# Six extra products on TensorE behind the fourth up-projection slab, in two layers and a third block

## The chip, the cores and the metric

The kernel runs on one NeuronCore of one Trainium2 chip, as one program. The metric is the device time of one execution in microseconds (us); where several executions were timed, their median is given.

## What is computed

The reference is a chain of three transformer blocks on 256 tokens of width 1024, all in 32-bit floats. The first block function runs its layer twice; the second one runs a different layer once, which the kernel calls the third block. Cut to what matters for the change:

```python
def first_block(x, mem, ...):
    for l in range(2):
        a = hybrid_mixer(rms_norm(x, pre_mix_g[l]), ...)
        x = x + rms_norm(a, post_mix_g[l])
        c = memory_cross_attention(rms_norm(x, pre_xattn_g[l]), rms_norm(mem, mem_g[l]), ...)
        x = x + rms_norm(c, post_xattn_g[l])
        hdn = jnp.square(jax.nn.relu(rms_norm(x, pre_mlp_g[l]) @ w_up[l]))      # 1024 -> 4096
        x = x + rms_norm(hdn @ w_down[l], post_mlp_g[l])                        # 4096 -> 1024
    return x

def second_block(x, mem, ...):
    ...
    h = rms_norm_2(x, norm_ffn_g[0])
    x = x + jnp.square(jax.nn.relu(h @ w_ff1[0])) @ w_ff2[0]                    # 1024 -> 4096 -> 1024
    return x
```

## The kernel before

Activations lie transposed: channels on the 128 partitions in eight chunks, the 256 tokens along the row. A weight matrix comes in slabs of 1 MB, 2048 floats on each partition, which are mostly eight 128-row chunks of 256 columns. There are 64 slabs to a layer and 59 in the third block. Slabs 32 to 47 of a layer are the up-projection and 48 to 63 the down-projection; in the third block these are 27 to 42 and 43 to 58.

To keep near 32-bit accuracy at the speed of the rounded type (F32R), each slab is split in two parts. SyncE loads the slab into one of two buffers `raw`, and waits for the low part of the slab two before. ScalarE copies it rounded into `w_hi` (`split_hi`, L504, the copy at L514), for which it waits until TensorE has done with the slab three before, since `w_hi` and `w_lo` are rings of three. VectorE writes the rest into `w_lo` (`split_lo`, L524). When that is done, the semaphore `slab_lo` is raised. The activations are split in the same way (`act_hi` and `act_lo`, for the hidden layer `h_hi` and `h_lo`, for an attention's output `o_hi` and `o_lo`).

TensorE then makes three products for each pair of chunks, high by high, high by low and low by high (`products3`, L560 to L562, within `columns_slab`; L2199, L2201 and L2203 for a down-projection slab). Each is one weight load of 128x128 and one product that streams 256 columns. A slab has 2 column halves x 8 chunks x 3 = 48 of them.

```python
def products3(pe, o, stat_hi, stat_lo, mov_hi, mov_lo, first, last):
    pe.matmul(o, stat_hi, mov_hi, start=first, stop=False)
    pe.matmul(o, stat_hi, mov_lo, start=False, stop=False)
    return pe.matmul(o, stat_lo, mov_hi, start=False, stop=last)
```

TensorE's program is in one order, written out by hand: `TE_ORDER` for a layer and `TE_ORDER_2` for the third block. In a layer the piece that matters here reads: slabs 28 to 31 (the last projection of the cross attention), `stat` 4, `pair` 32 (slabs 32 and 33 interleaved chunk by chunk, L603, L605 and L611), `stat` 5 (sums for the norm, L2061), and then slabs 34 to 63 without anything between them, and `stat` 6 (L2046). In the third block it is `pair` 27, `stat` 2, slabs 29 to 50, `out` 0 (four transposes of the result, L2378), slabs 51 to 54, `out` 1, slabs 55 to 58, `out` 2 and 3. Each item opens a bank of PSUM by `open_bank` (L542), which waits until the reader of the bank's use eight before has emptied it; the fifth up-projection slab writes the bank called `up4`.

Ahead of some items `keep_clock` (L2015, from the tables `WARM` and `WARM_2`) puts products whose result nobody reads. They multiply the identity by constants, both from the tile `cst`, in plain 32-bit floats, not in F32R:

```python
pe.matmul(b[:, 0:T], ident, cst[:, 0:T], start=True, stop=True)
```

VectorE scales an up-projection bank (L1444, `probs`), ScalarE squares it and rounds it (L929, L930), and VectorE writes `h_lo` (L1450).

Of the kernel before, what the change touches and what calls it, by code (L numbers as in the profile page):

```python
# [16 lines left out]
P = 128  # L17
T = 256
# [4 lines left out]
DEPTH = 2  # L23
# [295 lines left out]
def build(nc, A, out):  # L319
    ctx = ExitStack()  # L320
    with ctx:
        def sem(name):
            return ctx.enter_context(nc.semaphore(name))

        def sb(name, shape, dt=F32, on=ctx):
            return on.enter_context(nc.sbuf_tensor(name, shape, dt))
# [3 lines left out]
        w_hi = sb("w_hi", [P, RING, SLAB], F32R)  # L330
# [47 lines left out]
        sig = {name: sem(name) for name in PER}  # L378
# [17 lines left out]
        def value(name, layer, n):  # L396
            return layer * PER[name] + (n + (PER[name] if name in CREDIT else 0))
# [103 lines left out]
        def slot(layer, s):  # L501
            return (64 * layer + s) % RING
# [14 lines left out]
        def split_lo(dve, layer, s):  # L517

            dve.wait_ge(sig["slab_hi"], value("slab_hi", layer, s + 1))
            sp = s if s < 64 else 0  # L520
            pieces = split_views_2 if second(layer) else split_views
            for (d, r), (h, _) in zip(pieces(sp, w_lo[:, slot(layer, s)], raw[:, s % RAW]),
                                      pieces(sp, w_hi[:, slot(layer, s)], raw[:, s % RAW])):
                ins = dve.tensor_tensor(d, r, h.bitcast(F32), ALU.subtract)  # L524
            ins.then_inc(sig["slab_lo"], 1)
# [9 lines left out]
        def second(layer):  # L535

            return isinstance(layer, int) and layer == DEPTH

        def bank(use, layer=0):
            return banks[(INDEX_2 if second(layer) else INDEX)[use] % N_BANKS]  # L540

        def open_bank(pe, layer, use):  # L542

            n = (INDEX_2 if second(layer) else INDEX)[use] - N_BANKS
            if second(layer) and n >= 0:
                _, name, count = USES_2[n]
                if name in once:
                    pe.wait_ge(once[name], count)
                else:
                    pe.wait_ge(sig[name], value(name, DEPTH, count))  # L550
                return bank(use, layer)
            while USES[n % NU] is None:
                n -= N_BANKS
            _, name, count = USES[n % NU]
            pe.wait_ge(sig[name], value(name, layer, count - (PER[name] if n < 0 else 0)))
            return bank(use, layer)
# [1423 lines left out]
        def _(pe):  # L1980
# [21 lines left out]
            for l in range(DEPTH):  # L2002
# [5 lines left out]
                      start=True, stop=True).then_inc(i_turned, 1)  # L2008
# [6 lines left out]
            def keep_clock(layer, use, n):  # L2015

                b = open_bank(pe, layer, use)
                for _ in range(n):
                    pe.matmul(b[:, 0:T], ident, cst[:, 0:T], start=True, stop=True)

            def stat(layer, n):

                b = open_bank(pe, layer, f"stat{n}")
                if n == 1:
                    pe.wait_ge(sig["c_square"], value("c_square", layer, 1))
                    for half, (k0, k1) in enumerate(((0, 3), (3, 5))):
                        for k in range(k0, k1):
                            ins = pe.matmul(b[:, T * half:T * half + T], ones[:, :], kx_t[:, k, :],
                                            start=k == k0, stop=k == k1 - 1)
                    ins.then_inc(sig["stat_mm"], 1)  # L2030
                    return
                if n == 0 and layer:
                    sum_new_tokens(layer - 1, b, 6, True)
                elif n in (3, 5):
                    sum_new_tokens(layer, b, n - 1, False)
                else:
                    sum_tokens(layer, b, n - (n > 1), n == 0)

            def sum_tokens(layer, b, norm, both):

                pe.wait_ge(sig["sumsq"], value("sumsq", layer, 2 * norm + 2))
                parts = [(src, a) for src in (sumsq, sq_next) for a in range(2)]
                for n, (src, a) in enumerate(parts):
                    if n == 2:
                        pe.wait_ge(sig["square"], value("square", layer, 4 * norm + 4))
                    ins = pe.matmul(b[:, 0:T], ones[:, :], src[:, T * a:T * a + T], start=n == 0, stop=n == 3)  # L2046
                if both:
                    for i in range(TI):
                        for n, (src, a) in enumerate(parts):
                            ins = pe.matmul(b[:, T + i:T + i + 1], src[:, T * a + P * i:T * a + P * i + P],  # L2050
                                            ones[:, 0:1], start=n == 0, stop=n == 3)
                ins.then_inc(sig["stat_mm"], 1)

            def sum_new_tokens(layer, b, norm, both):

                pe.wait_ge(sig["eps_sq"], value("eps_sq", layer, norm // 2))
                parts = [eps_tile] + [qk_dil[:, k, :] for k in (0, 1, 4, 5)]
                for n, src in enumerate(parts):
                    if n in (1, 3):
                        pe.wait_ge(sig["sumsq"], value("sumsq", layer, 2 * norm + (n + 1) // 2))  # L2060
                    ins = pe.matmul(b[:, 0:T], ones[:, :], src, start=n == 0, stop=n == 4)  # L2061
                if both:
                    for i in range(TI):
                        for n, src in enumerate(parts):
                            ins = pe.matmul(b[:, T + i:T + i + 1], src[:, P * i:P * i + P], ones[:, 0:1],
                                            start=n == 0, stop=n == 4)
                ins.then_inc(sig["stat_mm"], 1)
# [158 lines left out]
            def rest_of(layer, s):  # L2226
                pe.wait_ge(sig["o_lo"], value("o_lo", layer, 8))
                half_slab(pe, layer, s, bank(slab_banks(s)[0][0]), o_hi, o_lo, 1)

            steps = {"half": half, "rest": rest_of, "slab": slab, "pair": pair, "stat": stat, "kpe": kpe, "scores": scores, "turn": turn, "pv": pv, "ot": turn_o}  # L2230
            for layer in range(DEPTH):
                for kind, n in TE_ORDER:
                    if (kind, n) in WARM:
                        keep_clock(layer, *WARM[kind, n])
                    steps[kind](layer, n)

            def stat_2(n):
# [232 lines left out]
            for kind, n in TE_ORDER_2:  # L2470
                if (kind, n) in WARM_2:
                    keep_clock(DEPTH, *WARM_2[kind, n])
                steps_2[kind](n)


# [15 lines left out]
```

## Time and profile before

| | |
|---|---|
| time, median of 3 executions | 1379.42 us (1376.05 to 1381.72) |
| the profiled execution's own time | 1372.25 us |
| its span, first to last instruction | 1370.2 us |
| TensorE products (PE), busy | 1306.6 us, 95% of the span, 10351 products |
| TensorE weight loads (PEld), busy | 1261.5 us, 92% |
| VectorE, ScalarE, GpSimd, busy | 833.6 us (61%), 666.7 us (49%), 90.0 us (7%) |
| transfers | 202.92 MB, 148 GB/s over the span |
| mean granted TensorE clock | 0.983 of full |
| longest shares of the chain that ended last | PE 76%, DVE 10%, ACT 7%, DMA 3%, issue 3% |

Times are from the start of the span. A product's duration in the profile runs from its start until its last result has left the array, so that it overlaps the next ones: how fast a stream of products runs is read from the distance between starts, or from two starts and the number of products between them. The granted clock is given as a share of 2.4 GHz; it has two levels, 1.00 and 0.50 (1.2 GHz).

### The profile page before, as it was taken

To read this page: it belongs to the slowest core of one execution; us is meant where nothing else is said; L and a number is where in the kernel's file an instruction comes from. 1 tells how busy PE (TensorE), PEld (TensorE's weight loads), DVE (VectorE), ACT (ScalarE), POOL (GpSimd) and SP (SyncE) were. 2 spreads that over 40 slices of the span, in tenths; PEclk is the share of its full clock that TensorE was granted. 3 is DMA by queue.
4 is the path that set the end of the run, shared out by engine and by line. 5 is a ranking of instruction groups with operands and counts; after the bars stand their busy time and mean duration, and the time that the engine had idled before them with its cause. 6 is when DMAs were issued, how large, how long until landed. Compare 5 with 4: busy or idle time off the path is not lost.

```text
span 1370.2 us, 23668 instructions
## 1 busy us (share of the span) xinstructions
PE 1306.6 (95%) x10351; PEld 1261.5 (92%) x10351; DVE 833.6 (61%) x919; ACT 666.7 (49%) x946; POOL 90.0 (7%) x65
## 2 busy tenths in 40 slices
PE   4999999999999999989999999999989998999998
PEld 3989999989999998989998999999788887999998
DVE  5567537666654557654756765457658757676542
ACT  4456546456533446545545554344356544465332
POOL 3000001010000100001101000013000100100000
PEclk7999999999999999999999999999899999999999
DMA  6634443336555453345333665547332221366552
GB/s 190 222 99 134 145 161 131 105 124 219 185 185 185 143 154 97 124 137 170 124 110 117 205 195 188 187 139 220 109 108 78 89 97 62 124 193 207 185 185 93
DMA packets 195573, 202.92 MB, mean 148 GB/s; under 512 B 5716, under 2 KB 191847, under 8 KB 195471
## 3 DMA queue, kind: packets, MB, share of 16 engines
q1 hardware_dynamic: 192704, 194.82, 44.2%
q0 software_dynamic: 2464, 5.99, 1.5%
q8 instruction: 82, 1.34, 0.4%
q10 hardware_dynamic: 303, 0.61, 0.2%
q14 instruction: 20, 0.16, 0.0%
HBM read 200.33 MB, written 3.16 MB: 149 GB/s over the span
## 4 chain that ended last, share of the span: by engine, by line
PE 76%; DVE 10%; ACT 7%; DMA 3%; issue 3%; POOL 1%; SPq 0%; DVEq 0%; ACTq 0%; POOLq 0%
PE bank L560 12%; PE bank L561 12%; PE bank L562 12%; PE bank L2203 7%; PE bank L2199 7%; PE bank L2201 7%; DVE w_lo L524 4%; ACT w_hi L514 3%; PE bank L603 2%; PE bank L605 2%; PE bank L611 2%; PE bank L2116 2%; PE bank L2100 1%; DMA raw<-in_w_in_dram 1%; DVE head_sq L1634 1%
## 5 line engine op out<-in xcount | busy, mean ns | idle before, releaser
L524 DVE TENSOR_TENSOR w_lo<-raw,w_hi 128x2048 fp32r<-128x2048 f32 (+7 forms) x210 | 424.0, 2029 | 372.5 <-ACT w_hi L514 372.2
L514 ACT ACTIVATE w_hi<-raw 128x2048 fp32r<-128x2048 f32 (+7 forms) x210 | 354.8, 1703 | 393.0 <-PE bank L2203 141.7
L560 PE MATMUL bank<-act_hi,w_hi 128*128 128x256 f32 x1096 | 310.0, 283 | 0.5 <-DVE w_lo L524 0.5
L562 PE MATMUL bank<-act_hi,w_lo 128*128 128x256 f32 x1096 | 307.1, 280 | 0.0
L561 PE MATMUL bank<-act_lo,w_hi 128*128 128x256 f32 x1096 | 307.1, 280 | 0.0
L2199 PE MATMUL bank<-h_hi,w_hi 128*128 128x256 f32 x768 | 215.7, 281 | 0.0
L2203 PE MATMUL bank<-h_hi,w_lo 128*128 128x256 f32 x768 | 215.6, 281 | 0.0
L2201 PE MATMUL bank<-h_lo,w_hi 128*128 128x256 f32 x768 | 215.5, 281 | 0.0
L560 PEld LDWEIGHTS bank<-act_hi,w_hi 128*128 128x128 f32 x1096 | 206.8, 189 | 1.3 <-issue 0.6
L561 PEld LDWEIGHTS bank<-act_lo,w_hi 128*128 128x128 f32 x1096 | 207.2, 189 | 0.3
L562 PEld LDWEIGHTS bank<-act_hi,w_lo 128*128 128x128 f32 x1096 | 207.1, 189 | 0.0
L2201 PEld LDWEIGHTS bank<-h_lo,w_hi 128*128 128x128 f32 x768 | 145.3, 189 | 0.0
L2203 PEld LDWEIGHTS bank<-h_hi,w_lo 128*128 128x128 f32 x768 | 145.3, 189 | 0.0
L2199 PEld LDWEIGHTS bank<-h_hi,w_hi 128*128 128x128 f32 x768 | 145.0, 189 | 0.0
L560 PE MATMUL bank<-o_hi,w_hi 128*128 128x256 f32 (+1 forms) x356 | 100.9, 283 | 2.4 <-issue 1.4
L561 PE MATMUL bank<-o_lo,w_hi 128*128 128x256 f32 (+1 forms) x356 | 99.9, 281 | 0.0
L562 PE MATMUL bank<-o_hi,w_lo 128*128 128x256 f32 (+1 forms) x356 | 99.8, 280 | 0.0
L753 POOL TENSOR_TENSOR sumsq<-sumsq,sq_next 128x512 f32<-128x512 f32 x18 | 43.5, 2419 | 817.9 <-ACT sq_next L871 817.9
L560 PE MATMUL bank<-w_hi,act_hi 128*128 128x256 f32 (+2 forms) x320 | 92.2, 288 | 0.9 <-DVE w_lo L524 0.9
L562 PE MATMUL bank<-w_hi,act_lo 128*128 128x256 f32 (+2 forms) x320 | 90.4, 282 | 0.0
L561 PE MATMUL bank<-w_lo,act_hi 128*128 128x256 f32 (+2 forms) x320 | 90.3, 282 | 0.0
L603 PE MATMUL bank<-act_hi,w_hi 128*128 128x256 f32 x280 | 70.0, 285 | 6.6 <-ACT act_hi L856 4.9
(354 smaller groups left out, 2178.4 us busy)
## 6 DMA issues: line engine op xcount, KB each, us to landing
raw<-in_w_up_dram SPq DMA_DIRECT2D x32, 1024.0 KB, 5.4
raw<-in_w_down_dram SPq DMA_DIRECT2D x32, 1024.0 KB, 5.2
raw<-in_w_ff_dram SPq DMA_DIRECT2D x32, 1024.0 KB, 5.4
raw<-in_w_in_dram SPq DMA_DIRECT2D x23, 1024.0 KB, 5.4
raw<-in_w_xk_dram SPq DMA_DIRECT2D x8, 1024.0 KB, 5.2
raw<-in_w_xv_dram SPq DMA_DIRECT2D x8, 1024.0 KB, 5.6
raw<-in_w_mix_out_dram SPq DMA_DIRECT2D x8, 1024.0 KB, 5.1
raw<-in_w_xq_dram SPq DMA_DIRECT2D x8, 1024.0 KB, 5.1
```

The costliest lines, as they stand in the source:

```text
L514: ins = act.activation(d, r, ACT.Copy)
L524: ins = dve.tensor_tensor(d, r, h.bitcast(F32), ALU.subtract)
L560: pe.matmul(o, stat_hi, mov_hi, start=first, stop=False)
L561: pe.matmul(o, stat_hi, mov_lo, start=False, stop=False)
L562: return pe.matmul(o, stat_lo, mov_hi, start=False, stop=last)
L603: pe.matmul(dst, stat_hi, mov_hi, start=k == 0 and opens, stop=False, skip_group_check=True)
L605: pe.matmul(dst, stat_lo, mov_hi, start=False, stop=False, skip_group_check=True)
L611: ins = pe.matmul(dst, stat_hi, mov_lo, start=False, stop=k == 7, skip_group_check=True)
L753: pool.tensor_tensor(sumsq[:, :], sumsq[:, :], sq_next[:, :], ALU.add)\
L2199: ins = pe.matmul(b[:, T * m:T * m + T], wh[:, k, cs], h_hi[:, 8 * c + k], start=c == 0 and k == 0 and m == 0, stop=False, skip_group_chec ...
L2201: pe.matmul(b[:, T * m:T * m + T], wh[:, k, cs], h_lo[:, 8 * c + k], start=False, stop=False, skip_group_check=True)
L2203: ins = pe.matmul(b[:, T * m:T * m + T], wl[:, k, cs], h_hi[:, 8 * c + k], start=False, stop=c == 3 and k == 7, skip_group_check=True)
```

## The change

A new function makes six products ahead of slab 36 of each layer and ahead of slab 31 of the third block, which is the fifth up-projection slab in all three. Stationary operand and streamed operand are parts of the same slab of `w_hi`: for k = 0 to 5 its columns 256k to 256k+127 against its columns 256k to 256k+255. All six write the first half of bank `up4`, each with `start=True`, so that the slab's own first product writes over them. The function waits for what the slab behind it waits for.

```diff
+            def weights_first(layer, s, use):
+
+                b = open_bank(pe, layer, use)
+                pe.wait_ge(sig["slab_lo"], value("slab_lo", layer, s + 1))
+                w = w_hi[:, slot(layer, s)]
+                for k in range(6):
+                    pe.matmul(b[:, 0:T], w[:, T * k:T * k + P], w[:, T * k:T * k + T], start=True, stop=True)
+
...
                     if (kind, n) in WARM:
                         keep_clock(layer, *WARM[kind, n])
+                    if (kind, n) == ("slab", 36):
+                        weights_first(layer, 36, "up4")
                     steps[kind](layer, n)
...
                 if (kind, n) in WARM_2:
                     keep_clock(DEPTH, *WARM_2[kind, n])
+                if (kind, n) == ("slab", 31):
+                    weights_first(DEPTH, 31, "up4")
                 steps_2[kind](n)
```

TensorE's instructions in a layer, at the seam of slab 35 (bank 7) and slab 36 (bank 0), before:

```order
L560 MATMUL bank7<-act_hi,w_hi 128x256
L561 MATMUL bank7<-act_lo,w_hi 128x256
L562 MATMUL bank7<-act_hi,w_lo 128x256
L560 MATMUL bank0<-act_hi,w_hi 128x256 [waits slab_lo,a_evac]
L561 MATMUL bank0<-act_lo,w_hi 128x256
```

The same place with the change (L2027 is the new product, whose both operands are `w_hi`):

```order
L560 MATMUL bank7<-act_hi,w_hi 128x256
L561 MATMUL bank7<-act_lo,w_hi 128x256
L562 MATMUL bank7<-act_hi,w_lo 128x256
L2027 MATMUL bank0<-w_hi 128x256 [waits slab_lo,a_evac]
L2027 MATMUL bank0<-w_hi 128x256 x5
L560 MATMUL bank0<-act_hi,w_hi 128x256 [waits slab_lo,a_evac]
L561 MATMUL bank0<-act_lo,w_hi 128x256
```

Six products come between the two slabs, and the pair of waits stands ahead of them and again ahead of the slab. The third block's seam, slab 30 (bank 5) to slab 31 (bank 6), with the change:

```order
L562 MATMUL bank5<-act_hi,w_lo 128x256
L2027 MATMUL bank6<-w_hi 128x256 [waits slab_lo,b2_w_evac]
L2027 MATMUL bank6<-w_hi 128x256 x5
L560 MATMUL bank6<-act_hi,w_hi 128x256 [waits slab_lo,b2_w_evac]
L561 MATMUL bank6<-act_lo,w_hi 128x256
```

No other instruction of any engine moves.

## Rows read from the trace of the kernel before

**Rows 1.** The page: its first line, PE and granted clock in 40 slices of 34.3 us.

```profile
span 1370.2 us, 23668 instructions
...
PE   4999999999999999989999999999989998999998
...
PEclk7999999999999999999999999999899999999999
```

**Rows 2.** Busy time in stretches: us; PE, PEld, DVE, ACT, POOL (instructions); clock, DMA share, GB/s.

```profile
310.00:367.00 57.00, 57.00 (x486) 57.00 (x485) 38.47 (x33) 32.39 (x34) 0.00 (x0) 1.00 0.63 201
757.00:812.00 55.00, 55.00 (x469) 55.00 (x469) 36.34 (x33) 31.84 (x32) 0.00 (x0) 1.00 0.65 206
1210.00:1270.00 60.00, 60.00 (x512) 60.00 (x511) 40.89 (x36) 32.95 (x34) 0.00 (x0) 1.00 0.62 196
```

**Rows 3.** PE timeline: start us, duration us; first products of slabs and what ends them.

```profile
310.00 0.28 PE L560 MATMUL bank<-act_hi,w_hi 128*128 128x256 f32 x1
...
468.29 0.38 PE L2046 MATMUL bank<-sumsq,ones 128*128 128x256 f32 x1
...
752.93 0.28 PE L560 MATMUL bank<-act_hi,w_hi 128*128 128x256 f32 x1
...
911.23 0.38 PE L2046 MATMUL bank<-sumsq,ones 128*128 128x256 f32 x1
...
1206.94 0.28 PE L560 MATMUL bank<-act_hi,w_hi 128*128 128x256 f32 x1
...
1320.01 0.60 PE L2378 MATMUL bank<-cst,x_t 128*128 128x128 f32 x4
```

**Rows 4.** PE by line in five stretches: count, duration ns min/median/max, first and last start.

```profile
L560 PE MATMUL bank<-act_hi,w_hi x187: 281/281/282, 310.0 to 375.7; 128*128 128x256 f32 x187
...
L2199 PE MATMUL bank<-h_hi,w_hi x62: 276/276/277, 1321.2 to 1341.9; 128*128 128x256 f32 x62
...
L560 PE MATMUL bank<-o_hi,w_hi x63: 276/276/277, 631.5 to 652.6; 128*128 128x256 f32 x63
...
L560 PE MATMUL bank<-act_hi,w_hi x62: 276/276/277, 489.4 to 510.1; 128*128 128x256 f32 x62
...
L560 PE MATMUL bank<-o_hi,w_hi x31: 276/276/279, 1172.5 to 1182.7; 128*128 128x256 f32 x31
```

**Rows 5.** PE timeline of the second layer's slabs 20 to 23: first, third and last product.

```profile
631.18 0.28 PE L560 MATMUL bank<-o_hi,w_hi 128*128 128x256 f32 x1
...
631.42 0.28 PE L562 MATMUL bank<-o_hi,w_lo 128*128 128x256 f32 x1
...
652.84 0.28 PE L562 MATMUL bank<-o_hi,w_lo 128*128 128x256 f32 x1
```

**Rows 6.** PE timeline at the first layer's seam of slabs 34 and 35.

```profile
304.18 0.28 PE L562 MATMUL bank<-act_hi,w_lo 128*128 128x256 f32 x1
304.30 0.33 PE L560 MATMUL bank<-act_hi,w_hi 128*128 128x256 f32 x1
304.46 0.28 PE L561 MATMUL bank<-act_lo,w_hi 128*128 128x256 f32 x1
304.58 0.28 PE L562 MATMUL bank<-act_hi,w_lo 128*128 128x256 f32 x1
```

**Rows 7.** DVE timeline: low parts of slabs 35, 36, 37; 36 of layer 1; 31.

```profile
301.84 2.28 DVE L524 TENSOR_TENSOR w_lo<-raw,w_hi 128x2048 fp32r<-128x2048 f32 x1
...
305.25 2.29 DVE L524 TENSOR_TENSOR w_lo<-raw,w_hi 128x2048 fp32r<-128x2048 f32 x1 [0.53 <-ACT w_hi L514]
...
311.49 2.29 DVE L524 TENSOR_TENSOR w_lo<-raw,w_hi 128x2048 fp32r<-128x2048 f32 x1 [2.74 <-ACT w_hi L514]
...
748.58 2.29 DVE L524 TENSOR_TENSOR w_lo<-raw,w_hi 128x2048 fp32r<-128x2048 f32 x1 [1.06 <-ACT w_hi L514]
...
1201.85 2.29 DVE L524 TENSOR_TENSOR w_lo<-raw,w_hi 128x2048 fp32r<-128x2048 f32 x1 [0.23 <-ACT w_hi L514]
```

**Rows 8.** PE timeline: a run of keep_clock products, first layer.

```profile
282.68 1.46 PE L2019 MATMUL bank<-cst 128*128 128x256 f32 x6
```

## The prediction

> **What bounds the kernel now.** I read the page first. TensorE's row shows a nine in nearly every slice, and its granted clock is full in nearly all of them, 2.4 GHz [rows 1]. The added products stand in the up-projections, so I looked at busy time in stretches behind each of the three places next. TensorE is busy for the whole of each stretch, 57.00 of 57.00, 55.00 of 55.00 and 60.00 of 60.00 us, at clock 1.00, while VectorE has about a third of its time free and ScalarE over 40% [rows 2]. So here nothing but TensorE's own stream sets the end, and there is no gap that an added product could fill.
>
> Then the timeline of TensorE, since in a saturated engine the pace is all there is. From the first product of slab 36 at 310.00 to the sum of squares behind slab 63 at 468.29 lie 28 slabs of 48 products: 158.29 us over 1344, **117.8 ns** from one product to the next. The second layer has 911.23 - 752.93 = 158.30 us for the same 1344, and the third block 1320.01 - 1206.94 = 113.07 us for the 960 of slabs 31 to 50, again 117.8 ns [rows 3].
>
> But that is not the only pace of such a product. In slabs 20 to 23 of the second layer the third product starts at 631.42 and the 192nd at 652.84: 21.42 us over 189 steps, **113.3 ns** [rows 5]. By line, a product lasts 281 ns at the slow pace and 276 ns at the fast one, with hardly a nanosecond between smallest and largest, and the fast value also holds for slabs 51 to 54 of the third block [rows 4]. Operands of one shape, all at the full clock, run at either of two paces, and stay at it for slabs on end. The durations tell the state at a glance. Two places show a turn. At 304.30 the first product of slab 35 is stretched to 0.33 us, since the low part of that slab was ready only at 301.84 + 2.28 = 304.12; the steps are 0.12, 0.16 and 0.12 us there, and the stream goes on slowly [rows 6, 7]. At 631.18 a change of operands with no visible gap is followed by the turn to the fast pace [rows 5].
>
> **The change, part by part.** It removes and moves nothing. It adds 3 x 6 = 18 products with their weight loads, and three repeated pairs of waits.
>
> *The waits* cost nothing. Slab 36 of the first layer has its low part at 305.25 + 2.29 = 307.54 and is begun at 310.00, 2.46 us later. In the second layer it is 750.87 against 752.93, in the third block 1204.14 against 1206.94 [rows 3, 7]. The bank `up4` was freed by the reader of the use eight before, two projections or a norm earlier. Were this cover gone, the slab itself would have waited as long.
>
> *The products* lie on the path with nothing beside them: TensorE is the bound, and every slab behind them, the norm's sum, and at the end the output are later by what they take. No row has a product of `w_hi` with itself. Nearest in type and shape are the F32R products around them, at 117.8 ns, or 113.3 ns in the other state. The other bound is a product that also takes both operands from one tile, the keep_clock one, but in plain floats: (1.46 - 0.38)/5 = 0.216 us each, with 0.38 us as the duration of such a plain-float product [rows 3, 8]. I take 117.8 ns, because the type sets what streams through the array. So 18 x 0.1178 = **+2.1 us**, between +2.0 (at 113.3) and +3.9 (at 0.216).
>
> Two rules of the Trainium skill would make this smaller and simpler. Its page "TensorE: Matmul & The Clock Gate", section "Back-to-back issue gap", gives N/2.4 + 2.5 ns to a warm product; for 256 columns that is 109.2 ns, an estimate of 2.0 us for the eighteen. The trace does not bear it out: both paces lie above it. The section "Step-by-step: what each phase is for" says that streaming and weight loading have a read port each and do not take bandwidth from one another, by which the operands' place could not matter and the first rival below would not exist; the two paces in the rows leave that open.
>
> *What it pushes.* Behind the six, TensorE frees each slab 0.7 us later at each place. ScalarE, SyncE and VectorE are ahead of it: slab 37's low part is ready at 313.78 against a start at 310.00 + 5.65 = 315.65 [rows 3, 7]. They shift along, and no queue has anything to lose. Nothing is gained either: each later wait of TensorE waits for work that itself follows from TensorE's results. The sum against the profiled execution is 1372.25 + 2.1 = 1374.4 us. That execution was faster than all three timed ones, whose median is 1379.42, so for the measured time I take **1379.42 + 2.1 = 1381.5 us**.
>
> **The rivals.** *The products turn the pace.* All three places stand in a stream at the slow pace that holds until the next change of work [rows 3, 4], and behind the last late slab of the first layer [rows 6]. A product of the slab with itself changes what is read together, and might knock the stream into the fast pace, which then lasts. Each of the steps behind is then 117.8 - 113.3 = 4.4 ns shorter: 1344 x 4.4 = 5.95 us for a layer and 960 x 4.4 = 4.25 us for the third block (slabs 51 to 54 are fast already [rows 4]). All three give 16.15 us, less 2.0 for the products: -14.1 us, **1365.3 us**. For it: the pace is a state, not a property of the product, and was turned at 631.3 by nothing but other operands [rows 5]. Against it: in the stretches of rows 3 the operands change from `act` to `h` between slabs 47 and 48 (and 42 and 43) with no turn, and the 70 other seams pass with none. If only some turn: one layer -3.9 (1375.5), the third block alone -2.2, two layers -9.8 (1369.6), a layer and the third block -8.2 (1371.2).
>
> *The fast stretches behind are lost.* The paces look like a lottery at each restart. Shifting all that follows by 0.7 to 2.1 us could draw it again the wrong way. From the first place on some 1330 slab products of the trace last 275 to 278 ns; four stretches of about four slabs each hold over half of them [rows 4]. All slow would cost 1330 x 4.4 = 5.9 us, with the eighteen 8.0: **1387.4 us**. It decides if nearly all of them turn; over 0.5% it is only with more than 1080 of them. Against it: a redraw should go both ways. A lost window of full clock would add to it, but TensorE is never idle near the places [rows 2].
>
> *The eighteen cost nothing or do not run.* They stand in TensorE's order, so this has only the measurement's spread for it.
>
> **How the numbers follow.** About 0.5%, 6.9 us, is what a measurement of this kernel can tell from no change. No turn, +2.1 us: 0.49. All three turn, -14.1 us: 0.25. Some turn: 0.19, about half of it two places (past -0.5%) and half one place. The fast stretches lost: 0.07. So faster 0.25 + 0.10 + 0.01 for spread = 0.36; slower 0.07; the same 0.57. The likeliest case alone, with the three timed runs lying up to 3.4 us from their median, spans 1378 to 1385. The range must take in the case of all three turned, 1365.3 with part of its spread, and goes up to 1386, just short of the other rival: 1363 to 1386.
>
> **What would show it.** Right: a row of 18 products on the new line with starts 0.12 us apart, granted clock 1.00, durations of 281 ns in the slabs behind all three places, and 0.71 us more from the last product of the slab ahead to the end of the projections. The pace is turned if the slabs behind the place show 276 ns and 28 slabs take 152.3 in place of 158.3 us. The price of the six is wrong if their starts are 0.2 us apart. The second rival is right if slabs 20 to 23 of the second layer, or 51 to 54, show 281 ns. The forecast is wrong as a whole if the time is below 1372 or above 1386 us.

## The result and the profile after

The changed kernel takes 1362.37 us (median of 4 executions, 1354.62 to 1364.59) against 1380.33 us before (4 executions, 1376.05 to 1381.72). The ratio is **0.987, 95% interval 0.982 to 0.991**: 1.3% faster, where 0.2% slower was forecast and 1363 was the lower end of the range. It is the first rival's case: in the profiled execution all three places turned ("to turn" here is to change from the one pace to the other). The medians differ by 18.0 us where that rival gave 14.1; the interval, 12.4 to 24.8 us, holds both, and what made the other 4 us is not shown. The fastest of the four, 1354.62 us, also had the highest mean granted clock, 0.987, where the others had 0.978 to 0.980.

The new products first: TensorE's timeline around them in the first layer (start us, us, engine line op), then all eighteen by line (count, duration in ns min/median/max, first and last start).

```profile
310.75 0.28 PE L562 MATMUL bank<-act_hi,w_lo 128*128 128x256 f32 x1
310.87 0.88 PE L2027 MATMUL bank<-w_hi 128*128 128x256 f32 x6
311.58 0.29 PE L560 MATMUL bank<-act_hi,w_hi 128*128 128x256 f32 x1
311.70 0.28 PE L561 MATMUL bank<-act_lo,w_hi 128*128 128x256 f32 x1
311.83 0.28 PE L562 MATMUL bank<-act_hi,w_lo 128*128 128x256 f32 x1
311.94 0.28 PE L560 MATMUL bank<-act_hi,w_hi 128*128 128x256 f32 x1
```

```profile
L2027 PE MATMUL bank<-w_hi x18: 278/283/287, 310.9 to 1204.3; 128*128 128x256 f32 x18
```

From 310.87 to the slab's own first product at 311.58 lie 0.71 us: six steps of 0.118, the price that the forecast took. The next two steps are 0.12 and 0.13 us, and then the steps are 0.11. Here are the slabs behind the three places by line, the same lines as in [rows 4]:

```profile
L560 PE MATMUL bank<-act_hi,w_hi x189: 276/276/277, 311.9 to 375.9; 128*128 128x256 f32 x189
...
L560 PE MATMUL bank<-act_hi,w_hi x190: 276/276/276, 749.6 to 813.9; 128*128 128x256 f32 x190
...
L560 PE MATMUL bank<-act_hi,w_hi x186: 276/276/277, 1204.8 to 1267.7; 128*128 128x256 f32 x186
...
L2207 PE MATMUL bank<-h_hi,w_hi x254: 276/276/276, 376.9 to 462.9; 128*128 128x256 f32 x127
```

276 ns in all, where it was 281: the fast pace. The last line is the first layer's down-projection, fast up to its end. Next the first product of the slab behind each place in the timeline, and what ends the stream (the sum of squares, now L2054, and the transposes `out` 0, now L2388), which answer to [rows 3]:

```profile
463.93 0.38 PE L2054 MATMUL bank<-sumsq,ones 128*128 128x256 f32 x1
...
748.94 0.28 PE L560 MATMUL bank<-act_hi,w_hi 128*128 128x256 f32 x1
...
901.29 1.02 PE L2054 MATMUL bank<-sumsq,ones 128*128 128x256 f32 x4
...
1204.42 0.28 PE L560 MATMUL bank<-act_hi,w_hi 128*128 128x256 f32 x1
...
1313.24 0.38 PE L2388 MATMUL bank<-cst,x_t 128*128 128x128 f32 x2
```

The 28 slabs take 463.93 - 311.58 = 152.35 us for 158.29 [rows 3] and 152.35 for 158.30; the twenty of the third block take 108.82 for 113.07. That is 5.94 + 5.95 + 4.25 = 16.1 us won, less 2.1 for the eighteen.

The two profiled executions lie only 1372.25 - 1364.59 = 7.7 us apart, not 14. The rest is in a stretch that the change does not touch, from the end of the second layer to the third block's place: 302.4 us after, 295.7 before. Busy time over just this stretch (columns as in [rows 2]), of the kernel before and then of the changed one:

```profile
911.20:1206.90 295.70, 276.03 (x2028) 254.79 (x2027) 207.77 (x265) 146.73 (x258) 26.18 (x17) 0.97 0.36 111
```

```profile
901.30:1203.70 302.40, 283.02 (x2028) 259.32 (x2027) 209.42 (x265) 146.98 (x258) 24.24 (x17) 0.94 0.35 109
```

It holds the same 2028 products, at a mean granted clock of 0.94 for 0.97: the chip granted 1.2 GHz for longer in this execution. TensorE is busy for 7.0 us more. Full clock is missing for 0.06 x 302.4 = 18 us against 0.03 x 295.7 = 9, an estimate that counts TensorE's idle time too and is enough for the 6.7 us.

### The profile page after: what moved, and what is told of

Read it like the earlier page. It is cut to its first block, busy times and chain, and to the rows that moved or that the text cites. A ratio compares the mean times of both kernels' runs of the same rounds, so it can differ in the third digit from the quotient of the medians.

```text
span 1362.5 us, 23707 instructions
## 1 busy us (share of the span) xinstructions
PE 1299.0 (95%) x10369; PEld 1251.8 (92%) x10369; DVE 835.7 (61%) x919; ACT 667.2 (49%) x946; POOL 88.2 (6%) x65
## 4 chain that ended last, share of the span: by engine, by line
PE 78%; DVE 8%; ACT 7%; issue 3%; DMA 3%; POOL 1%; SPq 0%; DVEq 0%; ACTq 0%
PE bank L560 12%; PE bank L562 12%; PE bank L561 12%; PE bank L2209 6%; PE bank L2207 6%; PE bank L2211 6%; DVE w_lo L524 3%; ACT w_hi L514 3%; PE bank L603 3%; PE bank L611 2%; PE bank L605 2%; PE bank L2124 2%; PE bank L2019 1%; PE bank L2108 1%; ACT probs L917 1%
## 5 line engine op out<-in xcount | busy, mean ns | idle before, releaser
L514 ACT ACTIVATE w_hi<-raw 128x2048 fp32r<-128x2048 f32 (+7 forms) x210 | 355.3, 1705 | 378.1 <-PE bank L2211 118.3
L2207 PE MATMUL bank<-h_hi,w_hi 128*128 128x256 f32 x768 | 212.2, 276 | 0.0
L2211 PE MATMUL bank<-h_hi,w_lo 128*128 128x256 f32 x768 | 212.0, 276 | 0.0
L2209 PE MATMUL bank<-h_lo,w_hi 128*128 128x256 f32 x768 | 212.0, 276 | 0.0
```

The lines of the kernel that those rows point to most:

```text
L514: ins = act.activation(d, r, ACT.Copy)
L2207: ins = pe.matmul(b[:, T * m:T * m + T], wh[:, k, cs], h_hi[:, 8 * c + k], start=c == 0 and k == 0 and m == 0, stop=False, skip_group_chec ...
L2209: pe.matmul(b[:, T * m:T * m + T], wh[:, k, cs], h_lo[:, 8 * c + k], start=False, stop=False, skip_group_check=True)
L2211: ins = pe.matmul(b[:, T * m:T * m + T], wl[:, k, cs], h_hi[:, 8 * c + k], start=False, stop=c == 3 and k == 7, skip_group_check=True)
```

## The experiments

Every kernel here runs at the pace of its long streams, so each was judged by two things: its time, and the duration of a slab product behind the three places in its profile (281 ns slow, 276 fast). "Theory A" is that the six products act through their operands, "B" that any added product does it, "C" that it is a matter of chance, "D" of the moment at which a stream starts. A1, A2 and A3 are forms of A: both operands in one tile, streaming from the weights, and the relative addresses.

### Which products turn the pace

`own_pattern`, six products as the slab itself makes them:

```diff
-                for k in range(6):
-                    pe.matmul(b[:, 0:T], w[:, T * k:T * k + P], w[:, T * k:T * k + T], start=True, stop=True)
+                wl = w_lo[:, slot(layer, s)]
+                for k in range(2):
+                    c = slice(T * k, T * k + P)
+                    products3(pe, b[:, 0:T], w[:, c], wl[:, c], act_hi[:, k], act_lo[:, k], k == 0, k == 1)
```

> Six added products at the same three places, but in the slab's own pattern: high by high, high by low, low by high for two chunks, so that the stream continues without any new kind of operand pair. Theory A (what turns the pace is the unlike pair of operands): no turn, 281 ns in the slabs behind all three places, about 2.1 us over the kernel before. Theory B (any added product, by the shift in time it makes): the turn comes as in the changed kernel, 276 ns behind the places, about 14 us under the kernel before. Theory C (a lottery at each place): some of the three places turn, in other places in other executions.

Measured: ratio 1.001 (0.999 to 1.003), 1379.17 us, 281 ns behind all three places. Added products as such do not bring the fast pace. Theory B falls, and so does every explanation by the 0.7 us of shift.

`stream_act` streams `act_hi` past the same stationary parts; `act_self` takes both operands from `act_hi`; `swapped` exchanges the roles:

```diff
-                    pe.matmul(b[:, 0:T], w[:, T * k:T * k + P], w[:, T * k:T * k + T], start=True, stop=True)
+                    pe.matmul(b[:, 0:T], w[:, T * k:T * k + P], act_hi[:, k], start=True, stop=True)     # stream_act
+                    pe.matmul(b[:, 0:T], act_hi[:, k, 0:P], act_hi[:, k], start=True, stop=True)         # act_self
+                    pe.matmul(b[:, 0:T], act_hi[:, k, 0:P], w[:, T * k:T * k + T], start=True, stop=True) # swapped
```

> Six products that keep w_hi as the stationary operand but stream act_hi, so each is of a kind that the slab also has; only the sequence of three is broken. Theory A in its narrow form (both operands from the weight tile): no turn, 281 ns, 2.1 us over the kernel before. If it is the broken rhythm of three that turns the pace: 276 ns and about 14 us under the kernel before.

> Six products of act_hi with itself: both operands from one tile, but nothing is streamed from the weights. Theory A1 (what turns the pace is that both operands lie in one tile): 276 ns behind the places, about 14 us under the kernel before. Theory A2 (what turns it is streaming from w_hi, as the exchanged roles did at two of three places, after which the slab streams from act_hi again): 281 ns, 2.1 us over the kernel before.

> Six products with act_hi as the stationary operand and w_hi streamed, the roles exchanged. In the kernel before such a change of roles at slab 20 of the second layer was followed by the turn, and in the first layer it was not. If streaming from the weight tile is what turns the pace: 276 ns behind all three, about 14 us under the kernel before. If both operands must lie in one tile: 281 ns, 2.1 us over it. A mixture (one or two places) speaks for a lottery at the change of roles.

Measured: `stream_act` 1.002 (1.000 to 1.004) and `act_self` 1.001 (0.998 to 1.004), both with 281 ns behind all three places. But at the second layer's place of `act_self` the stream had been fast. Slab 35 ahead of it, the six, and the slabs behind it:

```profile
L560 PE MATMUL bank<-act_hi,w_hi x15: 276/276/276, 746.6 to 751.4; 128*128 128x256 f32 x15
...
751.70 0.88 PE L2027 MATMUL bank<-act_hi 128*128 128x256 f32 x6
...
L560 PE MATMUL bank<-act_hi,w_hi x163: 281/281/281, 752.4 to 809.7; 128*128 128x256 f32 x163
```

The low part of slab 36 was ready at 749.58, 2.1 us before the six, so nothing was late: six products of activations with themselves turned this stream from fast to slow. The other eight places of the three kernels that stream activations were slow ahead and stayed so.

`swapped`: 0.989 (0.985 to 0.993), 1363.18 us. The slabs behind its three places, by line:

```profile
L560 PE MATMUL bank<-act_hi,w_hi x179: 281/281/282, 311.9 to 374.8; 128*128 128x256 f32 x179
...
L560 PE MATMUL bank<-act_hi,w_hi x189: 275/276/277, 750.8 to 814.7; 128*128 128x256 f32 x189
...
L560 PE MATMUL bank<-act_hi,w_hi x177: 276/276/277, 1204.9 to 1264.7; 128*128 128x256 f32 x177
```

Two of three are turned here; its four timed executions (1361.5 to 1365.3 us) do not tell whether that is always so. Among these kernels, what `swapped` and the change share, and what the others lack, is that **weights are streamed** and then activations again; only these brought the fast pace. That both operands lie in one tile is not needed for that (`swapped`) and not enough (`act_self`).

The kernel has such a seam of its own: slab 19 streams weights past stationary activations, slab 20 streams attention outputs past stationary weights, with nothing between. In the nine traces of kernels with this layout, that seam is crossed 18 times; slabs 20 to 23 then show 276 ns in 12 of them. With `pad112` below, whose paces are the same, it is 14 of 20. In the trace before it was one of two. The four places with six products of the weights (three in the changed kernel, one in `first_layer_only` below) all turned, which a chance of 14 in 20 at each would also give about one time in four.

Streamed weights are not the only thing that turns a stream. Between slabs 50 and 51 of the third block stand the four transposes of `out` 0, products of `x_t` with the identity from `cst` that touch no weights, and behind slab 51's first product comes a step of 0.21 us. In seven of the nine traces slab 50 is slow, and in all seven slabs 51 to 54 are fast, also in the trace before [rows 4]; behind `out` 1 three of nine fast streams were slow again. Where the slabs' own products follow one another at full clock, with nothing else between, the nine traces have eight changes of the state, all at the seam of two slabs: seven of them with a step stretched to 0.16 us or more, like that of [rows 6], the eighth with one of 0.13 us (`stream_act`, 143.34 us). One more stretched step, of 0.16 us, changed nothing (`act_self`, 746.21 us). What no kernel here tests is six products that stream from a third tile.

### How many, and where

```diff
-                for k in range(6):
+                for k in range(1):      # one_product
+                for k in range(3):      # three
```

> One product of the weight slab with itself at each place in place of six. Theory A: one unlike product may do, 276 ns behind all three places, 16.15 us less 3 x 0.11 gives about 15.8 us under the kernel before, 1.7 us under the changed one. If the turn needs a run of unlike products: 281 ns and no change of time. Theory C: a mixture.

> Three products of the weight slab with itself in place of six. One product turned none of the three places in its profiled execution, and its times spread over 19 us. If the turn takes a run of such products to settle: between the two, some places turned, 1364 to 1378 us. If three are enough: all three turned, about 1.0 us under the changed kernel.

Measured: one product 0.997 (0.994 to 1.001), its ten executions from 1363.3 to 1382.0 us; three 0.994 (0.991 to 0.998), ten executions from 1360.0 to 1380.7. In both profiled executions, which were among the longer ones, all three places show 281 ns. The other executions speak for a draw in each of them when the products are few. The kernel before spreads too, by 11.7 and 15.9 us in the same two comparisons, in part with the granted clock; but `three` took 1364.20 us at a mean clock of 0.976, where seven executions of the kernel before took 1375.08 to 1381.93 at that clock, and 1380.69 us at 0.979. How many places were turned in the short ones was not seen, since only one execution of each is profiled. With six, all four executions are shorter than any of the kernel before on record (1366.24 us the lowest).

`first_layer_only`:

```diff
-                    if (kind, n) == ("slab", 36):
+                    if (kind, n) == ("slab", 36) and layer == 0:
...
-                if (kind, n) == ("slab", 31):
-                    weights_first(DEPTH, 31, "up4")
```

> The six products of the first layer alone. If the gain is the sum of three independent turns: 1344 x 4.4 ns - 0.7 us = 5.3 us under the kernel before (ratio 0.996), 276 ns in slabs 36 to 63 of the first layer and 281 ns behind the two other places. If a turn is carried over into later parts, more than that.

Measured: 0.996 (0.993 to 0.999), 276 ns behind the first layer's place and 281 behind the other two. That is the gain of one turned layer, and the turn is not carried over to the later places.

### Whether the layout decides

The next seven kernels change one number of the kernel before, the width of a small tile ahead of `act_hi`, which moves `act_hi` and every tile behind it against the weight tiles:

```diff
-        neg_max = sb("neg_max", [P, 48])
+        neg_max = sb("neg_max", [P, 128])
```

> The kernel before without any added product, but with the small tile neg_max widened from 48 to 128 floats on each partition, which moves act_hi and all that lies behind it from 192 to 512 bytes past a multiple of the weight tiles' addresses. Theory A3 (the pace depends on how the two read streams' addresses lie to one another): the share of fast slab products changes by much, toward either side, up to 6692 x 4.4 ns = 29 us less or 1825 x 4.4 ns = 8 us more. Theory D (it hangs on the moment at which a stream starts, and not on addresses): as before, 281 ns in the three long streams, no change of time.

> The kernel before with neg_max at 64 floats: act_hi and all behind it move by 64 bytes. 128 floats (a shift of 320 bytes) gave 120.0 ns in all streams and no fast one. If the pace goes by the shift modulo 256 bytes, this is the same as 320: 120.0 ns, about 1390 us.

> The kernel before with neg_max at 80 floats, a shift of 128 bytes. Theory A3 (relative addresses decide the pace): one pace for all long streams, which may be any of 113.3, 117.8, 120.0 ns or a new one. Theory D (the moment decides): as before, 281 ns in the three long streams.

> The kernel before with neg_max at 96 floats, a shift of 192 bytes. As for 80 floats: A3 says that the pace of all streams changes together, D that nothing does.

> The kernel before with neg_max at 112 floats, a shift of 256 bytes. If the pace goes by the shift modulo 256 bytes, everything is as before: 117.8 ns in the three long streams, fast stretches at other places, about 1379 us. If the period is longer, or it is no matter of addresses but of the size: another pace.

> The kernel before with neg_max at 56 floats, a shift of 32 bytes, between the layout with two paces (shift 0) and that with 120.0 ns (shift 64). Relative addresses as the cause: one of 113.3, 117.8, 120.0 ns or a mixture in the long streams; with 113.3 in all of them the time would be about 1378 - 16 = 1362 us without any added product.

> The kernel before with neg_max at 88 floats, a shift of 160 bytes, between the layout with 117.8 ns (shift 128) and that with 118 and 120 ns mixed (shift 192). As for 56 floats.

One view tells all of them apart: busy time in the stretch from 330 to 440 us, in the middle of the first layer's stream, where TensorE is never idle and its clock is 1.00. The number behind PE is how many products fell into these 110 us, with some three in flight at the edges. The changed kernel, for comparison:

```profile
330.00:440.00 110.00, 110.00 (x973) 110.00 (x972) 63.74 (x46) 52.57 (x45) 2.91 (x1) 1.00 0.61 200
```

`padded` (shift 320 bytes) and `pad80` (128), each its own trace:

```profile
330.00:440.00 110.00, 110.00 (x919) 110.00 (x919) 60.62 (x45) 50.06 (x44) 2.92 (x1) 1.00 0.59 189
```

```profile
330.00:440.00 110.00, 110.00 (x937) 110.00 (x936) 63.31 (x47) 50.07 (x44) 2.92 (x1) 1.00 0.60 192
```

Less the three in flight, 110 us over 970, 916 and 934 products are 113.4, 120.1 and 117.8 ns. All layouts, with the duration of a product in that stream (the pace of the seven shifted ones is the length of the first layer's slabs 36 to 63 over 1344 products):

| width of `neg_max` | shift, bytes | pace ns | duration ns min/median/max | ratio to before |
|---|---|---|---|---|
| 48 (before) | 0 | 117.8, or 113.3 | 281, or 276 | 1 |
| 56 | 32 | 118.3 | 277/280/285 | 1.005 (1.002 to 1.008) |
| 64 | 64 | 120.0 | 283/283/283 | 1.012 (1.006 to 1.019) |
| 80 | 128 | 117.8 | 279/279/279 | 1.001 (0.999 to 1.003) |
| 88 | 160 | 120.0 | 279/282/286 | 1.011 (1.005 to 1.016) |
| 96 | 192 | 118.7 | 279/281/285 | 1.009 (1.005 to 1.013) |
| 112 | 256 | 117.8 | 281/281/281 | 1.001 (0.998 to 1.003) |
| 128 | 320 | 120.0 | 283/283/283 | 1.013 (1.008 to 1.019) |

Moving tiles alone, with the same instructions in the same order, changes the pace of the long streams at five of the seven shifts. Shifts of 64 and 320 bytes agree, and so do 0 and 256, as a period of 256 bytes would have it; that is two pairs, not a proof of the period. None of the seven is faster than the layout of the kernel before, and those of 128 and 256 bytes cannot be told from it by the time.

The long streams are not all, though. With `pad80`, slabs 20 to 23, which stream attention outputs, are at the fast pace in both layers; the first layer's:

```profile
L560 PE MATMUL bank<-o_hi,w_hi x64: 276/276/277, 188.5 to 209.9; 128*128 128x256 f32 x64
```

So this layout has a fast pace for streamed activations as well. With `padded` every stream of activations at full clock lasts 283 ns a product.

> The changed kernel, six products at each of the three places, with neg_max at 128 floats (all activation tiles 320 bytes further), where every stream ran at 120.0 ns. If the six products only choose between paces that the layout allows: 120.0 ns behind all three places and 2.2 us over the padded kernel, about 1394 us. If they turn the pace by themselves, whatever the layout: 113.3 ns behind the places, (1344 + 1344 + 960) x 6.7 ns = 24 us under it.

> The changed kernel with neg_max at 80 floats (128 bytes further), where the slabs that stream activations ran at 117.8 ns and most that stream weights at 113.3. If a fast pace is open to the long streams there too, the six products turn them: about 1365 us. If the layout has only the slow one for them: 117.8 ns and about 1381 us.

The changed kernel, with its six products, in these two layouts:

```profile
L560 PE MATMUL bank<-act_hi,w_hi x157: 283/283/283, 313.8 to 369.9; 128*128 128x256 f32 x157
```

```profile
L560 PE MATMUL bank<-act_hi,w_hi x170: 280/280/280, 310.0 to 369.7; 128*128 128x256 f32 x170
```

`pad128_six` (the first) stays at 120.0 ns, ratio to the kernel before 1.014 (1.009 to 1.019), like `padded` without them (283 ns, 1.013). `pad80_six` stays at 117.8 ns, ratio 1.001 (0.999 to 1.003). Their stretches from 330 to 440 us hold 920 and 936 products, as `padded` and `pad80` do within one. The six do not make a pace. Where the layout has none but the 120.0 ns they are 2 us of work. But it is not enough either that the layout has a fast pace: in the trace of `pad80_six` slabs 20 to 23 of both layers and slabs 0 and 1 of the second layer show 276 ns, and still none of the three places turned. Why the six fail there is open.

No version here is faster than the changed kernel. Further places were not tried: a stretch of four slabs is worth 192 x 4.4 ns = 0.85 us at most, and its six products cost 0.7.

## Why the prediction was wrong, point by point

- **What bounds the kernel**: right. TensorE is busy without a gap behind each place, before and after, and the nanoseconds on a product's step come out whole in the length of each stretch.
- **The price of the eighteen**: right, 0.71 us at a place at 117.8 ns each. The bound of 0.216 us by the plain-float product was far off. The waits cost nothing.
- **The pace as a state**: right, and read from the trace before. The sizes in the first rival, 5.95 and 4.25 us, were measured as 5.94, 5.95 and 4.25, and its 1365.3 us is within 3 us of the median. That closeness is in part luck: both medians before, 1379.42 and 1380.33, are of a kernel that spreads over 16 us. One of that rival's side cases is off in the sum: a layer and the third block give -10.2 + 2.1 = -8.1 us, not -8.2.
- **The chance of the turn is the step that failed.** It was put at 0.25 for all three, against 0.49 for none, on the ground that the change of operands between slabs 47 and 48 and "the 70 other seams" passed with no turn. Those were the wrong seams to count. At all of them the slabs' own products follow one another, weights stationary and activations streamed, and `own_pattern` shows that six more of such products bring no turn. The seams to count were those with something unlike between. The trace before had two where weights are streamed ahead of activations (slabs 19 to 20), of which one was turned to the fast pace, and one with the transposes `out` 0, where the slow stream became a fast one [rows 4]; the forecast read the first of these and named the fast slabs 51 to 54, but gave neither a weight against the 70. Over ten traces the seams of slabs 19 to 20 show the fast pace 14 times in 20, and a run of six products of the weights has turned all of its four profiled places in this layout.
- **The stretches behind lost**: did not happen; slabs 20 to 23 of the second layer and 51 to 54 show 276 ns again. The rival's premise, that a fast stream can be turned slow, is true: `act_self` did it.
- **The skill's rule**, by the page "TensorE: Matmul & The Clock Gate" and its section "Step-by-step: what each phase is for", that loading weights takes no read bandwidth from streaming, was left open in the forecast. The padded kernels show that where the operands lie does change the pace, 117.8 against 120.0 ns; so streaming and loading are not independent of each other's addresses here, or both depend on something else that moves with these tiles. The trace does not tell which. The 109.2 ns that the forecast took from the page's section "Back-to-back issue gap" were reached in no layout; the page gives that formula for an isolated product and not for a stream of weight load and product pairs, so the forecast set it against the wrong thing.

What stays open: why streaming weights moves the stream from one state to the other, why transposes and late operands do so too and in both directions, what a single product lacks that six have, why the six fail in the layout of `pad80`, and which pair of addresses matters, since the padding moved all tiles behind `neg_max` together.

## What to carry to other kernels

Where one engine is saturated, read the pace of its stream (start to start) and the duration's minimum, median and maximum per stretch before costing any edit: two values a few nanoseconds apart, each holding for hundreds of instructions, are a state that an edit can switch, and 1344 instructions at 4.4 ns are worth more than anything in the edit itself. When the evidence for such a switch is counted from the trace, count only the seams that resemble the edit in what is streamed and what is stationary, in both directions, and read the state ahead of the seam as well as behind it. And when a kernel's time moves by a per cent after an edit of a tile's size or order, compare the pace of its unchanged streams first.

## What the runs showed of the hardware that was not expected

- The same F32R products of 128x128 by 256 columns, at 2.4 GHz throughout, run at 113.3, 117.8, 118.3, 118.7 or 120.0 ns from start to start, depending on the layout of the tiles and, in the layout of this kernel, on which of two states the stream is in.
- Widening a tile of 192 bytes on each partition, which no product reads, by 64 bytes made the kernel 1.2% slower (1.006 to 1.019).
- In this layout a run of six products that stream from the weight tile was followed by the fast pace at four of four places (products of the weights with themselves) and at two of three (roles exchanged). Six that stream activations brought it at none of eight slow places, and at the ninth, where the stream was fast, they were followed by the slow one.
- Other things turn a stream too: four transposes ahead of slab 51, with a step of 0.21 us, were followed by the fast pace in seven of seven slow streams, and a step stretched by some 0.05 us, behind a late operand, turned the first layer's stream from fast to slow [rows 6].
